# Attention's steps laid between the matmuls of the query projection and of w_out's gating half

## The reference, cut to what matters

```python
# one layer, prompt part; the sample part is alike, with cached keys
xn = rmsnorm(xp, norm_mix[l])
q, k, v, qi, ki, wi, u, gv = project(xn, w_in[l], pos_p)       # one projection, split, rope
# index: relu(qi . ki) per head, weighted by wi, summed over 8 heads; top 128 keys (sample: 48)
a = dsa_prompt(q, qi, wi, k, v, ki, pos_p)                     # 8 heads of 64, 2 kv heads, softmax over the chosen keys
gvn = rmsnorm(gelu(gv), gate_norm[l])
bmix = gelu(u) * spatial_prompt(gvn, w_spatial[l], b_spatial[l])
xp = xp + concatenate([a, bmix], axis=-1) @ w_out[l]
xp = xp + sq_relu_ffn(rmsnorm(xp, norm_ffn[l]), w_ff1[l], w_ff2[l])
```

## Time and profile before

| what | value |
|---|---|
| runs of the kernel, us | 1472.02, 1470.62, 1513.19; median 1472.02 |
| span of the profiled execution, us | 1508.3 |
| time of the profiled execution | not listed; the run of 1513.19 is 4.9 above its span |
| TensorE, VectorE, ACT, POOL busy, share of the span | 98%, 44%, 35%, 12% |
| mean granted clock of TensorE, share of 2.4 GHz | 0.919 |
| DMA, mean | 68 GB/s |

### The profile page before, as it was taken

The page is one execution under the profiler, slowest core; times in us unless marked ns, Lnnn a source line. Parts: engine busy times, 40 slices in busy tenths (PEclk is TensorE's granted clock), DMA queues, the critical chain, the costliest instruction groups (busy, mean ns, idle before and its releaser), DMA issues.

```text
span 1508.3 us, 22280 instructions
## 1 busy us (share of the span) xinstructions
PE 1483.1 (98%) x9329; PEld 1323.6 (88%) x9329; DVE 664.4 (44%) x1172; ACT 521.8 (35%) x956; POOL 185.1 (12%) x215
## 2 busy tenths in 40 slices
PE   6999999999999999999999999999999999999997
PEld 5766766899999999999976677669999999999997
DVE  5257632245444444444623683213454444344453
ACT  5365542233213223133335553323332231321322
POOL 4246200020000000000214540000100000000011
PEclk8999755799999999999999995559999999999998
DMA  6211200033232222222321120001322222222221
GB/s 180 70 57 43 74 5 0 0 85 85 85 84 78 82 80 85 84 84 83 104 82 45 40 78 25 5 1 42 85 75 82 83 84 84 85 85 85 82 59 63
DMA packets 169252, 102.37 MB, mean 68 GB/s; under 512 B 6920, under 2 KB 159424, under 8 KB 169152
## 3 DMA queue, kind: packets, MB, share of 16 engines
q1 hardware_dynamic: 169152, 100.94, 23.0%
HBM read 96.98 MB, written 3.95 MB: 67 GB/s over the span
## 4 chain that ended last, share of the span: by engine, by line
PE 97%; DVE 1%; DMA 1%; ACT 1%; issue 0%; SPq 0%; DVEq 0%; ACTq 0%
PE bank L1334 61%; PE bank L1108 15%; PE bank L1219 6%; PE bank L1255 4%; PE bank L1235 3%; PE bank L1126 2%; PE bank L1270 2%; PE bank L1286 1%; PE bank L1140 1%; DMA late<-in_x_prompt 1%; PE bank L1200 1%; PE bank L1353 0%; PE bank L1069 0%; PE bank L1085 0%; ACT L677 0%
## 5 line engine op out<-in xcount | busy, mean ns | idle before, releaser
L521 ACT ACTIVATE ring_hi<-ring_raw 128x1024 fp32r<-128x1024 f32 x176 | 184.8, 1050 | 305.4 <-PE bank L1334 248.6
L1334 PE MATMUL bank<-vh,ring_hi 128*128 128x288 f32 x1280 | 275.4, 296 | 0.0
L1334 PE MATMUL bank<-vl,ring_hi 128*128 128x288 f32 x1280 | 275.2, 296 | 0.0
L1334 PE MATMUL bank<-vh,ring_lo 128*128 128x288 f32 x1280 | 275.2, 296 | 0.0
L766 DVE TENSOR_TENSOR ring_lo<-ring_raw,ring_hi 128x1024 fp32r<-128x1024 f32 x164 | 213.6, 1302 | 132.5 <-ACT ring_hi L521 125.5
L1334 PE MATMUL bank<-xh,ring_hi 128*128 128x288 f32 x1024 | 220.8, 297 | 0.0
L1334 PE MATMUL bank<-xl,ring_hi 128*128 128x288 f32 x1024 | 220.2, 296 | 0.0
L1334 PE MATMUL bank<-xh,ring_lo 128*128 128x288 f32 x1024 | 220.2, 296 | 0.0
L1334 PEld LDWEIGHTS bank<-vh,ring_hi 128*128 128x128 f32 x1280 | 205.2, 189 | 0.0
L1334 PEld LDWEIGHTS bank<-vh,ring_lo 128*128 128x128 f32 x1280 | 205.2, 188 | 0.0
L1334 PEld LDWEIGHTS bank<-vl,ring_hi 128*128 128x128 f32 x1280 | 205.2, 189 | 0.0
(11 more groups left out here) (161 smaller groups left out, 1608.9 us busy)
## 6 DMA issues: line engine op xcount, KB each, us to landing
ring_raw<-in_w_ff SPq DMA_DIRECT2D x128, 512.0 KB, 4.1
ring_raw<-in_w_in SPq DMA_DIRECT2D x32, 512.0 KB, 3.7
ring_raw<-in_w_out SPq DMA_DIRECT2D x16, 512.0 KB, 4.2
late<-in_x_prompt SPq DMA_DIRECT2D x4, 512.0 KB, 5.7
out_y_prompt<-late SPq DMA_DIRECT2D x4, 512.0 KB, 2.9
w_sp<-in_w_spatial SPq DMA_DIRECT2D x2, 512.0 KB, 4.2
gate_bc<-in_gate_norm SPq DMA_DIRECT2D x2, 256.0 KB, 4.9
out_k_prompt<-z SPq DMA_DIRECT2D x2, 256.0 KB, 4.3
```

What stands on the lines that cost most here:

```text
L521: s.activation(ring_hi[:, n % NSLOT, :], ring_raw[:, n % NRAW, :], ACT.Copy).then_inc(hi_ready, 1)
L1334: last = mm(bank[2 * (u % 4) + half][:, 0:HALF], w[:, k, :], a[:, k, HALVES[half]], start=k == order[0] and w is wh and a is ah, stop=k == ...
```

## The change

Attention no longer stands after the projection. The layer is written as a row of ticks, and tables (`PE_AT`, `ACT_AT`, `DVE_AT`, `POOL_AT`) say what each engine does in which tick. In ticks 0 to 139 TensorE does six projection matmuls (`unit_tick`), in ticks 140 to 171 six matmuls of w_out's gating half (`wb_tick`), and after them whatever the table puts into the tick; ticks 172 to 211 hold only such inserts. VectorE fills each tick up to 900 units with top-k steps (a step counts its keys plus 128).

- Projection: eight chunks of 256 columns in two halves of the contraction; after the first chunk (index queries, in two halves, ahead of tick 0) a unit is one tile of one chunk, four ticks long, in one of two PSUM banks. The query chunks come last, tile by tile.
- Index scores and attention go by pairs of heads in different row groups of the array, into a pair of banks: `index` every two ticks from 19 to 49, `scores` every 2.5 ticks from 120 to 167, with the transposes of the weights five ticks and the weighted sum seven ticks later. Scores are three fp32r matmuls on high and low parts of query and key.
- Spatial mixing stands in ticks 80 to 96, the gate's transposes eight ticks later. Spatial results and the transposes of query and output share bank 7, in turn (`last_bank`).
- VectorE weights and adds the index heads (`index_add`), makes all low parts of weights, and adds w_out's gating half into x (`wb_add`); the attention half of w_out follows as eight units of 24 matmuls. POOL keeps the rope, the gate's product and the sums of squares.
- At the start the first half-chunk waits for four low parts of x, the second for eight.
- The outputs of keys, values and gate are issued on SP's queue between the two loads of the first query chunk, behind waits for `roped` and `gvn_ready`.

```diff
-    C_Q, C_K = 0, DA
-    C_SMALL = DA + 2 * DKV + NIH * ID
+    C_K = DA
+    C_QI = DA + 2 * DKV
+    C_SMALL = C_QI + NIH * ID
...
+    CW = 256
+    CHUNKS = [C_QI, C_K, C_GV, C_GV + CW, C_U, C_U + CW, 0, CW]
+    QI, KV, GV0, GV1, U0, U1, Q0, Q1 = range(8)
+    NC = len(CHUNKS)
+    ZW = 2 * DKV + NIH * ID + NSM
...
     TILE_ORDER = [0, 1, SMP] + list(range(2, NPT))
-    ITEMS = [(t, h) for t in TILE_ORDER for h in range(NH)]
+    PAIRS = NH // 2
+    ITEMS = [(t, j) for t in TILE_ORDER for j in range(PAIRS)]
     NI = len(ITEMS)
     INDEX_TILES = TILE_ORDER[1:]
-    INDEX = [(t, h) for t in INDEX_TILES for h in range(NIH)]
...
+    SEQ_UNITS = [(QI, t) for t in range(NT)] + [(KV, t) for t in range(NT)]
+    SEQ_UNITS += [(c, t) for c in (GV0, GV1, U0, U1) for t in TILE_ORDER]
+    SEQ_UNITS += [(c, t) for pair in (TILE_ORDER[:2],) for c in (Q0, Q1) for t in pair]
+    SEQ_UNITS += [(c, t) for t in TILE_ORDER[2:] for c in (Q0, Q1)]
+    POS = {ct: n for n, ct in enumerate(SEQ_UNITS)}
+    NU = len(SEQ_UNITS)
+    NB = NU - NT
...
+    def unit_end(ct):
+        return 4 * (POS[ct] - NT + 1)
+    def ready_q(a):
+        return max(unit_end((Q0, TILE_ORDER[a])), unit_end((Q1, TILE_ORDER[a])))
+    ITEM_AT = [ready_q(0) + 8 + (5 * i) // 2 for i in range(NI)]
+    TR_AT = [15, 15, 16, 16, 26, 27, 28, 29]
+    INDEX_AT = [19 + 2 * p for p in range(NX)]
+    Q_BACK = [max(ready_q(a) + 5, ITEM_AT[PAIRS * (a - 1) - 1] + 1 if a >= 2 else 0) for a in range(NT)]
+    MIX_AT = [unit_end((U1, t)) - 4 for t in TILE_ORDER]
...
+    for n in range(2, S_OUT):
+        c = n // 2
+        if n >= NSLOT:
+            free = 0 if c - 2 == QI else max(unit_end((c - 2, t)) for t in range(NT))
+            at(ACT_AT, free + 1 + n % 2, "split", n)
+            at(DVE_AT, free + 2 + n % 2, "split", n)
...
+    for p, g in enumerate(INDEX_AT):
+        at(PE_AT, g, "index", p)
+        at(ACT_AT, g + 1, "index_relu", p)
+        at(DVE_AT, g + 2, "index_add", p)
...
+        at(DVE_AT, unit_end((GV1, TILE_ORDER[-1])) + 6 + a, "gv_norm", a)
+        at(PE_AT, MIX_AT[a], "spatial", a)
+        at(DVE_AT, MIX_AT[a] + 1, "mix_copy", a)
+        at(POOL_AT, MIX_AT[a] + 5, "gate", a)
+        at(PE_AT, MIX_AT[a] + 8, "gate_tr", a)
+        at(ACT_AT, MIX_AT[a] + 9, "gate_high", a)
+        at(DVE_AT, MIX_AT[a] + 10, "gate_low", a)
...
+        at(PE_AT, Q_BACK[a], "q_tr", a)
+        at(ACT_AT, Q_BACK[a] + 1, "q_high", a)
+        at(DVE_AT, Q_BACK[a] + 2, "q_low", a)
...
+    for i, g in enumerate(ITEM_AT):
+        at(PE_AT, g, "scores", i)
+        at(DVE_AT, g + 1, "masked", i)
+        at(ACT_AT, g + 2, "exp", i)
+        at(PE_AT, g + 5, "p_tr", i)
+        at(ACT_AT, g + 6, "p_copy", i)
+        at(PE_AT, g + 7, "weighted", i)
...
-        POOL_SPLITS = range(S_OUT - 2, S_OUT + NSLOT)
-        STEPS_PER_GROUP = 3
...
+                def index_add(p):
+                    t, h0 = INDEX[p]
+                    rows = ROWS[t]
+                    dve.wait_ge(idx_relu, NX * l + p + 1)
+                    for e in range(2):
+                        part, w = rl[0:rows, p % 2, e, 0:KEYS[t]], wi[0:rows, t, h0 + e:h0 + e + 1]
+                        if h0 + e == 0:
+                            ins = v.tensor_scalar(score[t][0:rows, :], part, w, None, ALU.mult)
+                        else:
+                            dve.wait_ge(idx_acc, 2 * (NX * l + p) + e)
+                            ins = v.scalar_tensor_tensor(score[t][0:rows, :], part, w, score[t][0:rows, :], ALU.mult, ALU.add)
...
+                budget = 0
+                for tick in range(G_LAST):
+                    budget = min(budget, 0) + 900
+                    for kind, i in DVE_AT.get(tick, ()):
+                        if kind == "split":
+                            split_lo(N0 + i)
+                            budget -= 1300
+                        elif kind == "small_fm":
...
+                    while budget > 0:
+                        cost = topk_next(tick)
+                        if not cost:
+                            break
+                        budget -= cost
...
+                def project(out, n, t, ks, first, final):
+                    wh, wl = (b.rearrange("p (k n) -> p k n", k=KH) for b in slot(n))
+                    for k in ks:
+                        kx = KH * (n % 2) + k
                         for a, b in ((xh, wh), (xh, wl), (xl, wh)):
...
+                                      stop=final and k == ks[-1] and a is xl)
+                    return last
+                def unit_tick(g):
+                    b, part = divmod(g, 4)
+                    c, t = SEQ_UNITS[NT + b]
+                    if part == 0:
+                        pe.wait_ge(proj_evac, NU * l + (NT + b - 1 if b >= 2 else b + 1))
+                    last = project(bank[b % 2][0:ROWS[t], 0:CW], 2 * c + part // 2, t, [2 * (part % 2), 2 * (part % 2) + 1],
+                                   part == 0, part == 3)
+                    if part == 3:
                         last.then_inc(proj_done, 1)
...
+                def wb_tick(g):
+                    w, part = divmod(g - G_WB, 2)
+                    j, half = divmod(w, 2)
+                    if w == 0 and part == 0:
+                        pe.wait_ge(gate_lo, NT * (l + 1))
+                    if part == 0 and w < 2:
+                        pe.wait_ge(proj_evac, NU * l + NU - 1 + w)
+                    elif part == 0:
+                        pe.wait_ge(wb_added, NWB * l + w - 1)
+                    wh, wl = (b.rearrange("p (k n) -> p k n", k=KH)[:, :, (j % 2) * P:(j % 2 + 1) * P] for b in slot(S_OUT + j // 2))
+                    for k in (2 * part, 2 * part + 1):
+                        for m, (b, a) in enumerate(((wh, vh), (wh, vl), (wl, vh))):
+                            last = mm(bank[(NB + w) % 2][:, 0:HALF], b[:, k, :], a[:, KH + k, HALVES[half]],
+                                      start=k == 0 and m == 0, stop=k == KH - 1 and m == 2)
+                    if part == 1:
+                        last.then_inc(wb_done, 1)
...
+                        if (c, h) == (6, 0):
+                            sp.wait_ge(roped, l + 1)
+                            zp = z[:, 0:NPT, :]
...
+                def scores_of(i):
+                    t, j = ITEMS[i]
+                    a, S = i // PAIRS, KEYS[t]
+                    if i == 0:
+                        pe.wait_ge(idx_relu, NX * (l + 1))
+                    if j == 0:
+                        pe.wait_ge(last_free, N7 * l + turn("q_tr", a) + 1)
...
+                        pe.wait_ge(masked, NI * l + i)
+                    kh, kl = (kTsh, kTsl) if t == SMP else (kTh, kTl)
+                    for m, (q_, k_) in enumerate(((qTh, kh), (qTl, kh), (qTh, kl))):
+                        for e in range(2):
+                            b = HD * e
+                            last = mm(pair[1][0:ROWS[t], e, 0:S], q_[b:b + HD, a % 2, j, 0:ROWS[t]], k_[b:b + HD, 0:S],
+                                      start=m == 0, stop=m == 2)
...
+                    pe.wait_ge(xl_ready, KT * 2 * l + KH * (h + 1))
+                    for t in range(NT):
+                        if h == 0 and l:
+                            pe.wait_ge(*unit_read(UNITS * l - 4 + t // 2))
+                        last = project(bank[t][0:ROWS[t], 0:CW], h, t, list(range(KH)), h == 0, h == 1)
...
+                for tick in range(G_LAST):
+                    if tick < G_WB:
+                        unit_tick(tick)
+                    elif tick < G_END:
+                        wb_tick(tick)
+                    for kind, i in PE_AT.get(tick, ()):
```

More of the change, by code:

```diff
@@ L90, in hybrid_encoder_program, with turn @@
+    for w in range(NWB):
+        at(DVE_AT, G_WB + 2 * w + 2, "wb_add", w)
+    LAST_BANK = [e for g in range(G_LAST) for e in PE_AT.get(g, ()) if e[0] in ("spatial", "q_tr", "o_tr")]
+    N7 = len(LAST_BANK)
+    def turn(kind, a):
+        return LAST_BANK.index((kind, a))
     ctx = ExitStack()
@@ L199, in hybrid_encoder_program @@
         vl = sb("vl", [P, KT, TOK], F32R)
[L201 removed]
+        pair = [ctx.enter_context(nc.psum_tensor(f"pair{i}", [P, 2, 512], F32)) for i in range(4)]
+        bank = [pair[i // 2][:, i % 2, :] for i in range(8)]
         w_ready = [sem(f"w_ready{s}") for s in range(NRAW)]
@@ L353, in _ @@
+                for h in (1, 0):
+                    for s in range(4):
+                        load(A["w_out"][l, h * KH * P:(h + 1) * KH * P, s * CW:(s + 1) * CW]
+                             .rearrange("(k p) n -> p k n", p=P), KH)
                 for g in range(GROUPS):
@@ L503, in _ @@
+                for tick in range(G_LAST):
+                    for kind, i in POOL_AT.get(tick, ()):
+                        if kind == "gate_newton":
+                            gate_newton(i)
+                        elif kind == "gate":
+                            gate(i)
+                        else:
+                            q_rope(i)
```

(25 more changed lines are left out.)

1014 lines of the change are left out of this document (507 added, 507 removed).

## The result

The changed kernel takes 1391.9 us (median of four runs, 1391.25 to 1393.62). The runs of the kernel before lie in two places, 1471 to 1478 us at a mean granted clock of 0.95 and 1505 to 1519 at 0.92, and the ratio is against the lower one, while the profile of before, and with it the forecast's sum, is of the upper one.

The account below looks back on a forecast made before the run. It took TensorE as the bound, a sixth of the span at half clock. Terms of -46.8 (layer 0) and -62.1 us (layer 1) took the span from 1508.3 to 1399.4, the time to 1404; range 1363 to 1460.

Parts of the forecast that it names:

- Prices: TensorE's instructions at full clock: 119 ns per 256-column matmul, 0.112 us per transpose, 0.105 per weighted sum, 1.06 per 512-key pair.
- The clock: Attention stage: 60.3 us instead of 124.6 and 130.1, -64.3 and -69.8, mostly from full clock, the rest from split scores.
- VectorE's waits: Second spatial matmul and first scores wait for VectorE's late queue: with small ones, 8 us of new waits per layer.
- Tail: After the last tick with matmuls, ACT and DVE steps follow one another: 4.6 us of waits per layer.
- Start: Layer 0 only: first matmul waits for four low parts of x, second half-chunk for all eight: +9.8 us.
- The other 4.9 us: Added to the forecast span of 1399.4: the slowest listed run, 1513.19, lies 4.9 us above its span of 1508.3.
- bunching: Rival: steps come late and bunch behind the matmuls, attention stands at the end again: 1471 us, no change; chance 0.06.
- VectorE as the bound: Rival: single-price top-k and no score-to-mask slack, 20 us waits per layer, 1432; chance 0.18 shared with matmul prices.
- the one that the prediction sets against the rule: Kernel before: full clock came up between 284 and 288 us in a run of transposes and weighted sums.

Follow-up runs that it names:

- bunched kernel with plain pairs: Changed kernel with w_out's gating half moved behind attention's steps and one plain fp32 score matmul per head, two heads still side by side: 1417.15 us.
- 1398 among the chunks: Changed kernel with one plain fp32 score matmul per head, two heads side by side, attention's steps still between groups of projection or w_out matmuls: 1398.27 us.
- bunched clock: Changed kernel with split scores kept and w_out's gating half 44 ticks later, so no such matmuls stand between attention's steps from tick 140: 1422.4 us.

## Why the prediction came out as it did

Layer 0 took 700.8 us from the span's start, 52.4 less than before (forecast 46.8); layer 1, to the end of its last FFN matmul, 672.6 against 737.5, 64.8 less (62.1).

- **Prices.** Right. 9.27/78 is 118.8 ns for 256 columns (119 taken). Transposes 0.88/8 = 0.110 (0.112), weighted sums 1.73/16 = 0.108 (0.105), spatial 2.00. A 512-key pair is 0.90 in the chain plus some 0.19 by which the next chunk is longer: 1.09 against 1.06, so index and score pairs run side by side as counted.
- **The clock**, the term of 64 and 70 us. Right in what it gave: 1.00 through the stage. What the forecast said of the reason holds, but wasn't whole. It credited the chunks between the steps; pairs of heads side by side bring most of it without them (1417 us bunched, 1398 among the chunks).
- **VectorE's waits**, 8 us per layer: right place, too large. 2.4 measured. The forecast let every late tick of VectorE's queue reach TensorE. The two runs with another share show why that was no idle worry: of the three shares tried, the waits are small at 900 only.
- **Tail**, 4.6 us per layer: 8.1/2 = 4.05. Not foreseen: the clock falls behind it and costs another 2.6 and 2.4 us, and the FFN's first product waits 1.2 for its low part.
- **Start**, +9.8: the second half of the first chunk began at 33.4 us instead of 36.4, but its 60 products and the row sums took 10.0 us where 60 x 0.119 + 1.0 are 8.1, since the clock was low there (0.84 from 33 to 44 us). So 1.1 less. This is the profiled execution's; others took 8.5 or 10.0 us there, and the part that is waited for came up to 3 us later.

For layer 0 that makes -1.1 - 5.6 - 0.5 + 2.6 + 1.2 = -3.4 against the forecast, and measured is -5.6; for layer 1 -5.6 - 0.5 + 2.4 + 1.2 = -2.5, and measured is -2.7. In layer 0 some 2 us are not accounted for. The other 4.9 us that the forecast had put between span and time, from the slowest run of before, were 1.9 in the profiled run, 3.0 less, and behind the last FFN matmul stand 16.6 us instead of 17.6. With the 5.6 and 2.7 that is the 12 us by which the forecast was too high.

Of the rivals, bunching was the one mispriced: 1471 in the forecast, 1422 when it was made, because pairs bring the clock back. VectorE as the bound (1432) was the nearest: a share of 600 gives 1447, one of 1300 gives 1423. The Trainium skill's rule (TensorE: Matmul & The Clock Gate, Part 4: PE-mode transpose) that the full clock doesn't engage for transposes speaks for a slow stage. Here the bunched kernel with plain pairs goes from 0.50 to 1.00 at about 222 us in a run of transposes, scores and weighted sums, and stays there from 225 to 283. So transposes among other matmuls don't keep the clock down; what a run of transposes alone would do, neither this run nor the one that the prediction sets against the rule shows.

## What to carry to other kernels

When TensorE is busy and half as fast, look at which matmuls fill the stretch before counting work. Here matmuls of other work between the steps were worth 70 us, and two half-height products side by side 51 beyond the work that they save; either was nearly enough. A wait can cost more than its length: behind this kernel's tail the clock fell and took 2.6 and 2.4 us more. Chunks held back for the tail covered both, which was worth 10 us. A fixed share for background work on an in-order queue can have a cliff on either side, at both of which others wait (here 55 us for a share of 600 and 31 for 1300): try it on both sides.

## What was not expected of the hardware

- A stretch of plain fp32 scores of one head on 64 rows, transposes and weighted sums stays at 0.50 with TensorE busy throughout (25.00 of 25.00 us from 225 to 250 us). With the second head on the other 64 rows the same stretch reads 1.00 with TensorE busy less (21.06 of 25.00). Whether it is the rows in use or the shorter scores that tells, these runs don't separate.
- With split scores the bunched clock fell a second time, to about 0.5 between some 244 and 254 us, and again in layer 1 (0.52 and 0.50 from 930 to 940 us), which the plain pairs didn't show (1422 against 1417). Why stays open.
- Where TensorE idled, the granted clock was often below 1.00 there or in what followed: 0.91 behind the tail, 0.75 from 120 to 150 us with the share of 1300 (18.37 of 30.00 us busy), 0.67 in the wait with 600. But not always: with plain pairs TensorE was busy for 5.8 of 9 us from 241 to 250 us, and the clock stayed at 1.00 there and behind it.
